# A two-layer streaming encoder on one core: reading o back before the last spill, per-chunk waits for q, and the norm roots of the first ConvFFN taken together

## The chip, the core and the metric

The kernel runs on one core of a Trainium2 chip. The metric is device time in microseconds of one execution of the whole program. Of the kernel before, three runs were timed. The core has TensorE for matmuls (PE, and PEld for its weight loads), VectorE (DVE), ScalarE (ACT), GpSimd (POOL) and SyncE (SP), each with its own instruction stream, executed in order. They wait for one another through semaphores only, and all waits are written by hand.

## The reference, cut to what matters

```python
D_MODEL, SEQ, DEPTH, DEC_SEQ, PAST_LEN = 1024, 1024, 2, 32, 256
N_HEADS, HEAD_DIM, D_FF = 16, 64, 2816

# layer 0: attention over a band of 9 chunks of 64 keys, with a relative bias
q, k, v = split(rms_norm(x, ln_mix) @ w_qkv)
o = softmax(q @ k.T * HEAD_DIM ** -0.5 + bias) @ v
x = x + o @ w_o
# layer 1 has a gMLP in its place: gelu(h @ w_in), a mix over 128 positions, @ w_out
# after either layer
a = rms_norm(x, ln_ffn) @ w_up                       # 1024 -> 5632
c = conv_b + sum(a[t - 2 + j] * conv_w[j] for j in 0, 1, 2)
gate, val = split(c)
x = x + (silu(gate) * val) @ w_down                  # 2816 -> 1024
# at the end: rms_norm(x, ln_final)
```

All data is float32. There are 1024 prompt rows and 32 sample rows. The outputs are y, the new K and V rows, the gMLP's v rows and the last rows before the convolution.

## The kernel before

**Layout.** x lies transposed in SBUF: 128 partitions, 8 feature tiles, 1056 columns (1024 prompt, 32 sample). The columns are cut into three chunks `CH` of 352 (c = 0, 1, 2). Every float32 product is made of three products of rounded parts: `product` (L158 to L160) multiplies hi by hi, lo by hi and hi by lo. `linear` runs it over 8 feature tiles, 24 matmuls of 352 columns for one output tile. The input of a matmul is `gx_hi` and `gx_lo`; weights arrive in `raw`, are rounded by ACT into `w_hi` and the rest is written by DVE into `w_lo` (a "split").

**Attention.** The 16 heads go in 8 pairs t = 0 to 7 (`PAIRS`, `LAST` = 7). Each pair has 9 steps s (`STEPS`): 8 blocks of 128 query rows and the sample block, and g = 9t + s counts all 72 steps (`ALL`). In step g PE does `scores(g)` (into PSUM banks 0 to 3), `weigh(g - 2)` (probabilities by v, into bank 6), `turn(g - 1)` (transposes of probabilities) and one output tile for the next pair, `projection(t, s)`, into bank 7. The nine tiles of a projection are v, k and q in that order, three chunks each (`divmod(s, NCH)`); DVE scales each into place and counts it in `lin_out`. The softmax of a step runs through DVE (`maxima`: bias, maximum), ACT (`exps`) and DVE (`scale`). ACT and DVE split the output o of a step into hi and lo (`high`, `low`; `low` counts `o_out`). PE waits for `lin_out` at STEPS * (t + 1) before `scores` of step 0 of a pair, that is, for all nine tiles.

**o on its way to Wo.** For pairs 0 to 6, POOL stores o_hi and o_lo into a scratch tensor in HBM, in three pieces of 384, 384 and 288 columns: `spill(t, i)` for i = 0, 1, 2. The last piece of a pair is stored at the start of the next pair's turn of the POOL loop. After the loop, `back(c)` for c = 0, 1, 2 reads the o of pairs 0 to 6 into tiles 0 to 6 of gx_hi and gx_lo, which the projections read until then; it waits for `qkv_done` (the last projection that reads chunk c) and for `spilled`. The o of pair 7 is written straight into tile 7. `back(c)` is two DMAs of 1.2 MB, counted in `o_back[c]`.

**Wo.** In pair 7 there is no next pair to project. From step 1 on, `filler(d)` computes one tile of o @ w_o for chunk 0 in that place, in bank 7; `filler(0)` first waits for `o_back[0]`. Fillers 0 to 3 leave tile 7 out, and `short(d)` adds it later. After the steps come the sixteen late tiles of chunks 1 and 2 (`for i in range(2 * KT)`), alternating banks 6 and 7, each added to x by DVE (`add`). Ahead of them PE waits for `o_out` at ALL, the lo part of the very last o. Bank 6 holds that o too. ACT and DVE write the norm's inputs of the finished x (`act_tile`, `dve_tile`), and POOL sums the squares.

**The first ConvFFN.** An iteration takes 4 weight units of 128 columns (u = 0 to 3: gate, value, gate, value) by 3 chunks: 12 "up" tiles into a ring of 6 banks, then 24 "down" tiles of 6 matmuls each. In the first iteration the tile order is (0,c0), (1,c0), (0,c1), (1,c1), (0,c2), (1,c2), (2,c0), (2,c1) and so on; o numbers them 0 to 11. For each up tile DVE evicts the bank (L1586, times rstd, counted in `free`), ACT and DVE compute the convolution (L1527, L1596, L1599), ACT takes the silu of a gate (L1532), DVE the product of a value (L1607), and both split it into h_hi and h_lo (L1488, L1564). A down chunk waits for its h_lo. rstd has to be made here: `nb_columns` on PE (sums over partitions, L300), `nb_inverse` on DVE with `nb_roots` on ACT in its middle (mean, square root, reciprocal, diagonal), `nb_spreads` on PE (L329), `nb_rstd` on ACT (L335); group 0 is the first half of the columns, group 1 the rest. The splits of units 2 and 3 and of the two down units (4, 5) are written into this order by the table `SPLITS`. In layer 0 the split of unit 2 is done at o = 0, that of unit 3 at o = 6.

## Time and profile before

| | us |
|---|---|
| runs, median (lowest to highest) | 2581.31 (2580.66 to 2583.95) |
| the profiled execution | 2582.81 |
| its span | 2581.0 |
| PE busy | 2504.8 (97%) |
| DVE busy | 1512.8 (59%) |
| ACT busy | 893.5 (35%) |
| POOL busy | 258.5 (10%) |

The profile is one execution. Its times count from the first instruction; the span leaves out 1.8 us around it. The chain of work that ended last lies on PE for 89% of the span, so the rows to read are those where PE waits and those of the granted clock: TensorE runs at one of two levels, 2.4 GHz (1.0) and 1.2 GHz (0.5), and over the whole span the mean was 0.988.

### The profile page before, as it was taken

To read this page: it belongs to the slowest core of one execution; us is meant where nothing else is said; L and a number is where in the kernel's file an instruction comes from. 1 tells how busy PE (TensorE), PEld (TensorE's weight loads), DVE (VectorE), ACT (ScalarE), POOL (GpSimd) and SP (SyncE) were. 2 spreads that over 40 slices of the span, in tenths; PEclk is the share of its full clock that TensorE was granted. 3 is DMA by queue.
4 is the path that set the end of the run, shared out by engine and by line. 5 is a ranking of instruction groups with operands and counts; after the bars stand their busy time and mean duration, and the time that the engine had idled before them with its cause. 6 is when DMAs were issued, how large, how long until landed. Compare 5 with 4: busy or idle time off the path is not lost.

```text
span 2581.0 us, 42736 instructions
## 1 busy us (share of the span) xinstructions
PE 2504.8 (97%) x16343; PEld 2427.8 (94%) x16343; DVE 1512.8 (59%) x2833; ACT 893.5 (35%) x1665; POOL 258.5 (10%) x569
## 2 busy tenths in 40 slices
PE   7999999979899999999999999999999999999998
PEld 7888888769899999999999899999999999999998
DVE  4555555556666666666665524244766666666666
ACT  5444444434522222223333530233323333222223
POOL 0111111112200000000000420221000000000003
PEclk9999999989999999999999999999999999999999
DMA  6122222264111111111111210111111111111012
GB/s 155 57 58 58 58 58 60 62 173 124 65 38 45 45 36 49 49 49 49 49 49 33 61 39 17 51 33 49 50 50 49 49 49 49 49 45 37 34 48 77
DMA packets 136980, 145.29 MB, mean 56 GB/s; under 512 B 4940, under 2 KB 126452, under 8 KB 136884
## 3 DMA queue, kind: packets, MB, share of 16 engines
q1 hardware_dynamic: 121844, 118.82, 14.4%
q0 software_dynamic: 14384, 23.03, 3.4%
q10 hardware_dynamic: 656, 2.12, 0.2%
q8 instruction: 66, 1.08, 0.2%
q14 instruction: 30, 0.25, 0.0%
HBM read 125.97 MB, written 17.97 MB: 56 GB/s over the span
## 4 chain that ended last, share of the span: by engine, by line
PE 89%; DVE 5%; ACT 3%; POOL 2%; issue 1%; DMA 1%; ACTq 0%; POOLq 0%; DVEq 0%
PE psum L158 26%; PE psum L160 26%; PE psum L159 26%; PE psum L996 2%; PE psum L1017 2%; PE psum L979 2%; POOL total L229 1%; PE psum L1848 1%; DVE gx_lo L217 1%; PE psum L898 0%; DVE w_lo L763 0%; ACT conv_t L1527 0%; ACT w_hi L759 0%; DVE gx_lo L2007 0%; PE psum L1836 0%
## 5 line engine op out<-in xcount | busy, mean ns | idle before, releaser
L158 PE MATMUL psum<-gx_hi,w_hi 128*128 128x352 f32 x3456 | 1132.9, 328 | 36.8 <-issue 12.6
L159 PE MATMUL psum<-gx_lo,w_hi 128*128 128x352 f32 x3456 | 1120.5, 324 | 0.0
L160 PE MATMUL psum<-gx_hi,w_lo 128*128 128x352 f32 x3456 | 1119.3, 324 | 0.0
L158 PEld LDWEIGHTS psum<-gx_hi,w_hi 128*128 128x128 f32 x3456 | 653.4, 189 | 42.9 <-issue 26.4
L159 PEld LDWEIGHTS psum<-gx_lo,w_hi 128*128 128x128 f32 x3456 | 654.0, 189 | 0.9 <-issue 0.7
L160 PEld LDWEIGHTS psum<-gx_hi,w_lo 128*128 128x128 f32 x3456 | 653.7, 189 | 0.0
L1623 DVE TENSOR_TENSOR x<-x,psum 128x352 f32<-128x352 f32 x528 | 258.9, 516 | 123.0 <-PE psum L160 123.0
L1527 ACT ACTIVATE conv_t<-a_gate,cur 128x352 f32<-128x352 f32 x132 | 90.2, 683 | 535.9 <-DVE a_gate L1586 535.6
L158 PE MATMUL psum<-h_hiA,w_hi 128*128 128x352 f32 x528 | 172.2, 326 | 4.3 <-DVE x L1623 4.3
L158 PE MATMUL psum<-h_hiB,w_hi 128*128 128x352 f32 x528 | 172.4, 327 | 0.0
L160 PE MATMUL psum<-h_hiB,w_lo 128*128 128x352 f32 x528 | 171.9, 326 | 0.0
L160 PE MATMUL psum<-h_hiA,w_lo 128*128 128x352 f32 x528 | 171.4, 325 | 0.0
L159 PE MATMUL psum<-h_loA,w_hi 128*128 128x352 f32 x528 | 170.6, 323 | 0.0
L159 PE MATMUL psum<-h_loB,w_hi 128*128 128x352 f32 x528 | 170.4, 323 | 0.0
L1411 DVE TENSOR_TENSOR w_lo<-raw,w_hi 128x1024 fp32r<-128x1024 f32 x132 | 161.0, 1220 | 11.0 <-ACT w_hi L1408 11.0
L1586 DVE TENSOR_TENSOR a_gate<-psum,rstd 128x352 f32<-128x352 f32 (+2 forms) x176 | 72.0, 430 | 143.3 <-PE psum L160 137.5
L1408 ACT ACTIVATE w_hi<-raw 128x1024 fp32r<-128x1024 f32 x132 | 136.0, 1044 | 5.6 <-DMA raw<-in_f_w_up 5.6
L1596 DVE SCALAR_TENSOR_TENSOR conv_t<-a_gate,cur,conv_t 128x352 f32<-128x352 f32 x132 | 77.4, 586 | 96.0 <-ACT conv_t L1527 95.8
L1527 ACT ACTIVATE conv_t<-a_val,cur 128x352 f32<-128x352 f32 x132 | 90.2, 683 | 101.8 <-DVE a_val L1586 101.8
L1532 ACT ACTIVATE s_gate<-conv_t 128x352 f32<-128x352 f32 x132 | 65.9, 499 | 165.1 <-DVE conv_t L1599 165.1
L1596 DVE SCALAR_TENSOR_TENSOR conv_t<-a_val,cur,conv_t 128x352 f32<-128x352 f32 x132 | 77.3, 586 | 72.0 <-ACT conv_t L1527 71.8
L1670 POOL COPY tails<-a_gate 128x2 f32 (+1 forms) x88 | 13.9, 190 | 928.5 <-DVE a_gate L1586 928.5
(189 smaller groups left out, 2989.3 us busy)
## 6 DMA issues: line engine op xcount, KB each, us to landing
raw<-in_f_w_up SPq DMA_DIRECT2D x44, 1024.0 KB, 5.0
raw<-in_f_w_down SPq DMA_DIRECT2D x22, 1024.0 KB, 4.8
raw<-in_a_w_o SPq DMA_DIRECT2D x25, 512.0 KB, 3.8
raw<-in_a_w_qkv SPq DMA_DIRECT2D x24, 512.0 KB, 3.7
raw<-in_b_w_in SPq DMA_DIRECT2D x8, 1024.0 KB, 5.5
raw<-in_b_w_out SPq DMA_DIRECT2D x4, 1024.0 KB, 5.2
gx_hi<-o_scratch POOLq DMA_DIRECT2D x3, 1232.0 KB, 10.7
gx_lo<-o_scratch POOLq DMA_DIRECT2D x3, 1232.0 KB, 12.9
```

Source lines behind the costliest of these rows:

```text
L158: pe.matmul(out, w[0], rhs[0], start=first, stop=False)
L159: pe.matmul(out, w[0], rhs[1], start=False, stop=False)
L160: return pe.matmul(out, w[1], rhs[0], start=False, stop=last)
L979: mm = pe.matmul(psum[:, 2 * h + i, :m], q_tok[par][HEAD_ROWS[h], P * s:P * (s + 1)], kT[par][HEAD_ROWS[h], first + m * i:first + m * (i + ...
L996: mm = pe.transpose(psum[:rows, GROUP_BANK[i], P * (2 * j + h):P * (2 * j + h + 1)], probs[g % 2][h][:, at:at + rows], ident[:, :])
L1408: act.activation(shape(f_hi[slot]), self.raw_of(u), ACT.Copy).then_inc(self.w_hi, 1)
L1411: dve.tensor_tensor(shape(f_lo[slot]), self.raw_of(u), shape(f_hi[slot]), ALU.subtract)\
L1527: act.activation(conv_t[:, o % 2, :m], a_buf[g][:, start + 2:start + 2 + m], ACT.Identity, scale=cur[:, 2, g, i:i + 1], bias=cur[:, 3, g, ...
L1532: act.activation(s_gate[:, start:start + m], conv_t[:, o % 2, :m], ACT.Silu).then_inc(self.silu, 1)
L1586: mm = dve.tensor_tensor(a_buf[g][:, at:at + b - a], psum[:, o % RING, a - start:b - start], rstd[:, a:b], ALU.mult)
L1596: dve.scalar_tensor_tensor(t, a_buf[g][:, start + 1:start + 1 + m], cur[:, 1, g, i:i + 1], t, ALU.mult, ALU.add).then_inc(self.conv1, 1)
L1623: mm = dve.tensor_tensor(chunk(x[:, d, :], c), chunk(x[:, d, :], c), psum[:, n % RING, :CH[c][1]], ALU.add)
```

## The change

The change touches five places.

- POOL: `back(0)` is issued in the turn of pair 6, after `spill(6, 1)`, and `back(1)` at the end of that turn, both ahead of `spill(6, 2)`. `back(2)` stays.
- PE: `scores` of a pair waits for the q of chunk 0 in step 0, for chunk 1 in step 2 and for chunk 2 in step 5.
- PE and DVE: the late Wo tiles take bank 7 first, then 6. The wait for `o_out` at ALL moves ahead of the second tile; the first waits for a smaller count before its last feature tile.
- The first ConvFFN, layer 0, norm: PE takes the column sums of group 0 at o = 2 (before: 4), spreads group 0 and sums group 1 at o = 4 (before: 5 and 6), spreads group 1 at o = 5 (before: 7). DVE makes both inverses ahead of the first eviction, and ACT both sets of roots.
- The same place, weights: unit 3 is split at o = 2 (before: 6).

```diff
--- before.py
+++ after.py
@@ -882,10 +882,13 @@
             pool.wait_ge(kv_copied, extras_to(g + 6))
             store_v(t + 1)
             spill(t, 1)
+            if t == LAST - 1:
+                back(0)
             pool.wait_ge(kv_copied, extras_to(g + 8))
             store_k(t + 1)
-        for c in range(NCH):
-            back(c)
+            if t == LAST - 1:
+                back(1)
+        back(2)
 
     def extra_pe(pe, e, par_next, bank):
         out = psum[:, bank, :]
@@ -921,6 +924,10 @@
     def first_extra(pe, n):
         at_least(pe, kv_copied, n - 1)
         extra_pe(pe, FIRST_EXTRAS[n], 0, 4 + n % 2)
+
+
+    QUERY_CHUNK = {0: 0, 2: 1, 5: 2}
+    assert all(P * (s + 1) <= CH[max(c for r, c in QUERY_CHUNK.items() if r <= s)][0] + 352 for s in range(NB))
 
     O_PIECE = [(0, 3 * P), (3 * P, 6 * P), (6 * P, TW)]
 
@@ -970,8 +977,8 @@
                     pe.matmul(psum[:, 2 * h, PAST:n], q_tok[par][HEAD_ROWS[h], SMP:], kT[par][HEAD_ROWS[h], SMP:],
                               start=True, stop=True).then_inc(qk_done, 1)
                 return
-            if s == 0:
-                pe.wait_ge(lin_out, STEPS * (t + 1))
+            if s in QUERY_CHUNK:
+                pe.wait_ge(lin_out, STEPS * t + 2 * NCH + QUERY_CHUNK[s] + 1)
             parts = 2 if n > BANK else 1
             m = n // parts
             for i in range(parts):
@@ -1087,15 +1094,20 @@
                     pe.wait_ge(kc_in, 16 * (t + 1))
                 extra_pe(pe, extra_at(g), (t + 1) % 2, 6)
 
-        pe.wait_ge(o_out, ALL)
         for i in range(2 * KT):
             n = WO + WO_ROWS + 1 + i
             c = 1 + i // KT
             if i % KT == 0:
                 pe.wait_ge(o_back[c], 32)
-            pe.wait_ge(at_added, max(KT, C0_DONE + i - 1) if i > 1 else KT)
+            if i == 1:
+                pe.wait_ge(o_out, ALL)
+            pe.wait_ge(at_added, C0_DONE + i - 1 if i > 1 else KT)
             pe.wait_ge(at_lo, n + 1)
-            linear(pe, psum[:, 6 + i % 2, :CH[c][1]], f_hi[unit_slot(n)], f_lo[unit_slot(n)], c).then_inc(wo_done, 1)
+            out, hi, lo = psum[:, 7 - i % 2, :CH[c][1]], f_hi[unit_slot(n)], f_lo[unit_slot(n)]
+            linear(pe, out, hi, lo, c, None, range(LAST), False)
+            if i == 0:
+                pe.wait_ge(o_out, STEPS * LAST + LAST_BLOCK[c] + 1)
+            linear(pe, out, hi, lo, c, None, range(LAST, KT)).then_inc(wo_done, 1)
 
     def attention_act(act, norm):
         act.wait_ge(qkv_done, 5)
@@ -1289,7 +1301,7 @@
                 ffn[0].split(None, dve, 0, 0)
             if i:
                 norm.dve_tile(dve, *divmod(i - 1, KT))
-            add(C0_DONE + i, 1 + i // KT, i % KT, 6 + i % 2)
+            add(C0_DONE + i, 1 + i // KT, i % KT, 7 - i % 2)
         norm.dve_tile(dve, 1, KT - 1)
         ffn[0].split(None, dve, 0, 1)
         for d in range(KT):
@@ -1413,6 +1425,7 @@
 
         SPLITS = {3: 2, 6: 3, 7: 4, 8: 5}
         NEXT_SPLITS = {2: 0, 7: 1}
+        EARLY_SPLITS = ((2, 3), (2,))
 
         def pe(self, pe, banks_free, beside=lambda e, n: None):
             ring = RING
@@ -1421,10 +1434,13 @@
                 done = self.done + it
                 for o, (u, c) in enumerate(self.items(first)):
                     if first and self.layer == 0:
-                        if o in (4, 6):
-                            nb_columns(pe, (o - 4) // 2)
-                        elif o in (5, 7):
-                            nb_spreads(pe, ((0,), (1, 2))[(o - 5) // 2])
+                        if o == 2:
+                            nb_columns(pe, 0)
+                        elif o == 4:
+                            nb_spreads(pe, (0,))
+                            nb_columns(pe, 1)
+                        elif o == 5:
+                            nb_spreads(pe, (1, 2))
                     elif first and o in self.norm_at:
                         stage = self.norm_at.index(o)
                         if stage == 0:
@@ -1493,18 +1509,20 @@
                 for o, (u, c) in enumerate(items):
                     g, i = u % 2, u // 2
                     start, n = CH[c]
-                    if o in self.SPLITS and not (first and self.SPLITS[o] == 2):
+                    if o in self.SPLITS and not (first and self.SPLITS[o] in self.EARLY_SPLITS[self.layer]):
                         self.split(act, None, it, self.SPLITS[o])
                     if o and items[o - 1][0] % 2:
                         value_hi(done, *items[o - 1])
                     if first and o == 0 and self.layer == 0:
                         nb_roots(act, 0)
                         nb_rstd(act, (0,))
+                        nb_roots(act, 1)
                         act.wait_ge(self.up, 2 * NCH - 1)
                         self.split(act, None, it, 2)
+                        nb_rstd(act, (1, 2))
                     elif first and o == 2 and self.layer == 0:
-                        nb_roots(act, 1)
-                        nb_rstd(act, (1, 2))
+                        act.wait_ge(self.up, 2 * NCH)
+                        self.split(act, None, it, 3)
                     elif first and o == 0:
                         self.norm_in.act_roots(act)
                         self.norm_in.act_spread(act, (0, 1, 2))
@@ -1573,8 +1591,9 @@
                     if first and o == 0 and self.layer == 1:
                         self.norm_in.dve_columns(dve)
                         self.split(None, dve, it, 2)
-                    if first and self.layer == 0 and o in (0, 2):
-                        nb_inverse(dve, o // 2)
+                    if first and self.layer == 0 and o == 0:
+                        nb_inverse(dve, 0)
+                        nb_inverse(dve, 1)
                     if first and self.layer == 0 and u == 0:
                         dve.wait_ge(nb_ready, 2 * c + 1 if c < 2 else 3)
                     elif first and u == 0:
@@ -1586,8 +1605,8 @@
                         mm = dve.tensor_tensor(a_buf[g][:, at:at + b - a], psum[:, o % RING, a - start:b - start],
                                                rstd[:, a:b], ALU.mult)
                     mm.then_inc(self.free, 1)
-                    if first and o == 0 and self.layer == 0:
-                        self.split(None, dve, it, 2)
+                    if first and o in (0, 2) and self.layer == 0:
+                        self.split(None, dve, it, 2 + o // 2)
                     if o and items[o - 1][0] % 2:
                         value_lo(done, *items[o - 1])
                     m = CONV_N[c]
@@ -1608,7 +1627,7 @@
                                                    conv_t[:, o % 2, cut.start - start:cut.stop - start],
                                                    s_gate[:, cut], ALU.mult)
                         mm.then_inc(self.prod, 1)
-                    if o in self.SPLITS and not (first and self.SPLITS[o] == 2):
+                    if o in self.SPLITS and not (first and self.SPLITS[o] in self.EARLY_SPLITS[self.layer]):
                         self.split(None, dve, it, self.SPLITS[o])
                 value_lo(done, *items[-1])
                 at_least(dve, self.added, DOWN * done)
```

In the rows of the order, line numbers after the change are 10 to 20 higher than before from the first ConvFFN on (L1408 is L1420, L1411 is L1423, L1527 is L1545, L1532 is L1550, L1564 is L1582, L1586 is L1605, L1596 is L1615, L1607 is L1626).

The order of POOL's DMAs from the third `store_k` row on, before and after (o_scratch<-o_hi 128x288 is `spill(6, 2)`, gx_hi<-o_scratch is a `back`):

```order
L843 DMA out_2<-kout 128x4x128
L845 DMA out_4<-kout 32x128
L853 DMA o_scratch<-o_hi 128x288
L853 DMA o_scratch<-o_lo 128x288
L834 DMA vc<-in_cache_a_v 128x2x128
L862 DMA gx_hi<-o_scratch 128x7x352
L862 DMA gx_lo<-o_scratch 128x7x352
L862 DMA gx_hi<-o_scratch 128x7x352
L862 DMA gx_lo<-o_scratch 128x7x352
L862 DMA gx_hi<-o_scratch 128x7x352
L862 DMA gx_lo<-o_scratch 128x7x352
```

```order
L862 DMA gx_hi<-o_scratch 128x7x352
L862 DMA gx_lo<-o_scratch 128x7x352
L843 DMA out_2<-kout 128x4x128
L845 DMA out_4<-kout 32x128
L862 DMA gx_hi<-o_scratch 128x7x352
L862 DMA gx_lo<-o_scratch 128x7x352
L853 DMA o_scratch<-o_hi 128x288
L853 DMA o_scratch<-o_lo 128x288
L834 DMA vc<-in_cache_a_v 128x2x128
L862 DMA gx_hi<-o_scratch 128x7x352
L862 DMA gx_lo<-o_scratch 128x7x352
```

Two of the three read-backs have moved ahead of the store of kout, and of the last spill with the load of vc.

ACT at the start of the first ConvFFN, before and after (L321 is a square root, w_hi<-raw a split, L335 rstd; the rows begin after the last square):

```order
L321 ACT_TABLE_LOAD
L321 ACTIVATE rs_col<-rs_col 128x4
L335 ACTIVATE rstd<-psum 128x512
L1408 ACTIVATE w_hi<-raw 128x1024
L1527 ACTIVATE conv_t<-a_gate,cur 128x352
L1532 ACT_TABLE_LOAD
L1532 ACTIVATE s_gate<-conv_t 128x352
L1527 ACTIVATE conv_t<-a_val,cur 128x352
L1488 ACTIVATE h_hiA<-prod 128x352
L321 ACT_TABLE_LOAD
L321 ACTIVATE rs_col<-rs_col 128x4
L321 ACTIVATE rs_col<-rs_col 32x1
```

```order
L321 ACT_TABLE_LOAD
L321 ACTIVATE rs_col<-rs_col 128x4
L335 ACTIVATE rstd<-psum 128x512
L321 ACTIVATE rs_col<-rs_col 128x4
L321 ACTIVATE rs_col<-rs_col 32x1
L1420 ACTIVATE w_hi<-raw 128x1024
L335 ACTIVATE rstd<-psum 128x512
L335 ACTIVATE rstd<-psum 128x32
L1545 ACTIVATE conv_t<-a_gate,cur 128x352
L1550 ACT_TABLE_LOAD
L1550 ACTIVATE s_gate<-conv_t 128x352
L1545 ACTIVATE conv_t<-a_val,cur 128x352
```

The second square roots now follow the first without a table load between, the split of unit 2 stands behind them and ahead of the second rstd.

DVE in the same place, from the first product (prod) on, before and after:

```order
L1607 TENSOR_TENSOR prod<-conv_t,s_gate 128x352
L307 TENSOR_SCALAR rs_col<-psum 128x4
L307 TENSOR_SCALAR rs_col<-psum 32x1
L311 RECIPROCAL rs_col<-rs_col 128x4
L311 RECIPROCAL rs_col<-rs_col 32x1
L315 TENSOR_SCALAR total<-ident,rs_col 128x128 x4
L315 TENSOR_SCALAR total<-ident,rs_col 32x32
L1586 TENSOR_TENSOR a_gate<-psum,rstd 128x352
L1564 TENSOR_TENSOR h_loA<-prod,h_hiA 128x352
L1596 SCALAR_TENSOR_TENSOR conv_t<-a_gate,cur,conv_t 128x352
```

```order
L1626 TENSOR_TENSOR prod<-conv_t,s_gate 128x352
L1605 TENSOR_TENSOR a_gate<-psum,rstd 128x352
L1423 TENSOR_TENSOR w_lo<-raw,w_hi 128x1024
L1582 TENSOR_TENSOR h_loA<-prod,h_hiA 128x352
L1615 SCALAR_TENSOR_TENSOR conv_t<-a_gate,cur,conv_t 128x352
```

The means, reciprocals and diagonals of group 1 are gone from here; the split of unit 3 (w_lo<-raw,w_hi) has come in behind the next eviction.

## Rows read from the trace of the kernel before

**Rows 1.** Page part 1, then waits of PE: waited for: us in total, times, longest.
```profile
PE 2504.8 (97%) x16343; PEld 2427.8 (94%) x16343; DVE 1512.8 (59%) x2833; ACT 893.5 (35%) x1665; POOL 258.5 (10%) x569
...
PE psum L158 <- issue: 12.6, 1, 12.6
...
PE psum L979 <- DVE q L1203: 5.0, 7, 0.7
```
**Rows 2.** Timeline of PE: start, duration, what, [idle before <- who ended it].
```profile
450.44 0.32 PE L160 MATMUL psum<-gx_hi,w_lo 128*128 128x352 f32 x1
450.68 0.49 PE L979 MATMUL psum<-kT,q 64*128 64x256 f32 x2
...
506.29 0.32 PE L160 MATMUL psum<-gx_hi,w_lo 128*128 128x352 f32 x1
507.32 0.49 PE L979 MATMUL psum<-kT,q 64*128 64x128 f32 x4 [0.71 <-DVE q L1203]
...
513.81 0.33 PE L996 MATMUL psum<-ident,pB 128*128 128x128 f32 x1
526.72 0.63 PE L158 MATMUL psum<-gx_hi,w_hi 128*128 128x352 f32 x1 [12.58 <-issue]
...
532.20 0.92 PE L979 MATMUL psum<-kT,q 64*128 64x384 f32 x4
```
**Rows 3.** Timeline of POOL's DMA issues around the read-back.
```profile
496.60 0.56 POOL L853 DMA_DIRECT2D o_scratch<-o_hi  x1 [11.02 <-DVE o_lo L1242]
...
518.12 0.96 POOL L862 DMA_DIRECT2D gx_lo<-o_scratch  x1
```
**Rows 4.** DMA issued from 518 to 519: KB each, median us to landing.
```profile
gx_lo<-o_scratch POOLq DMA_DIRECT2D x1, 1232.0 KB, 8.5
```
**Rows 5.** Stretches: us, PE, PEld, DVE, ACT, POOL busy (count), PE clock, DMA share, GB/s.
```profile
514.00:514.20 0.20, 0.14 (x1) 0.00 (x0) 0.20 (x1) 0.02 (x1) 0.00 (x0) 0.50 0.54 92
...
592.50:595.90 3.40, 3.40 (x13) 3.40 (x13) 0.13 (x1) 0.00 (x0) 0.00 (x0) 0.51 0.55 157
703.30:708.50 5.20, 5.20 (x18) 5.20 (x19) 3.66 (x7) 3.10 (x5) 0.43 (x3) 0.50 0.61 202
```
**Rows 6.** Timeline of DVE, then of PE, at the first late Wo tile.
```profile
588.29 1.23 DVE L763 TENSOR_TENSOR w_lo<-raw,w_hi 128x1024 fp32r<-128x1024 f32 x1 [2.22 <-ACT w_hi L759]
...
591.39 0.43 PE L158 MATMUL psum<-gx_hi,w_hi 128*128 128x352 f32 x1 [2.78 <-DVE gx_lo L1242]
```
**Rows 7.** Timeline of PE in the first ConvFFN iteration.
```profile
670.75 0.95 PE L300 MATMUL psum<-ones,total 128*128 128x2 f32 x8
671.55 0.41 PE L158 MATMUL psum<-gx_hi,w_hi 128*128 128x352 f32 x1
...
675.49 1.02 PE L329 MATMUL psum<-total,ones 128*128 128x512 f32 x2
...
680.21 1.10 PE L300 MATMUL psum<-ones,total 128*128 128x2 f32 x10
...
686.85 1.46 PE L329 MATMUL psum<-total,ones 128*128 128x512 f32 x4 [1.49 <-DVE total L315]
...
703.30 0.66 PE L158 MATMUL psum<-gx_hi,w_hi 128*128 128x352 f32 x1 [7.11 <-DVE w_lo L1411]
...
717.26 0.32 PE L158 MATMUL psum<-h_hiA,w_hi 128*128 128x352 f32 x1
```
**Rows 8.** Timeline of ACT: the split of unit 2, ahead of the first convolution.
```profile
677.04 1.05 ACT L1408 ACTIVATE w_hi<-raw 128x1024 fp32r<-128x1024 f32 x1
```
**Rows 9.** Timeline of DVE in the same iteration.
```profile
683.34 0.21 DVE L307 TENSOR_SCALAR rs_col<-psum 128x4 f32<-128x4 f32 x2
...
690.01 0.58 DVE L1596 SCALAR_TENSOR_TENSOR conv_t<-a_gate,cur,conv_t 128x352 f32<-128x352 f32 x1 [0.32 <-ACT conv_t L1527]
...
714.06 0.52 DVE L1564 TENSOR_TENSOR h_loB<-prod,h_hiB 128x352 fp32r<-128x352 f32 x1
...
721.65 0.94 DVE L1623 TENSOR_TENSOR x<-x,psum 128x352 f32<-128x352 f32 x2
```

## The prediction

> **What bounds the kernel now.** I read the page's busy shares first, then PE's list of waits, then the timeline of PE at each of them, and last the granted clock of the stretches around. PE is busy 97% of the span [rows 1], so only time in which PE stands still or runs at the lower clock can be won. The largest single wait is one of 12.6 us that the list puts down to "issue". The timeline has it at the first filler of pair 7: work on PE ends at 514.14 and goes on at 526.72 [rows 2]. What came just then is the second DMA of `back(0)`: issued at 518.12 [rows 3], landed 8.5 us later [rows 4], at 526.62. Next are 7 waits of 0.7 us for the last q tile, one for each pair from 1 to 7 [rows 1, 2], a wait of 2.78 us for the very last o_lo [rows 6], and two in the first iteration of the first ConvFFN, 1.49 us for the diagonals and 7.11 us for the w_lo of unit 3 [rows 7]. After three of these waits TensorE worked at 1.2 GHz for a while [rows 5]. All five parts of the change lie on one of these waits; nothing else of the program moves.
>
> **Read-back, at the start of pair 7.** `back(0)` needs the projection of chunk 0 (done well before pair 6's step 7) and the first piece, stored long before. So it is issued right behind `spill(6, 1)`, whose first DMA stands at 496.60 [rows 3]: two issues of 0.56 us, then two of 0.96. The last of these begins at about 498.7, and with the same 8.5 us to landing it is there at 507.2, while `filler(0)` could start at 513.9. Cover: 6.7 us; each microsecond of landing beyond costs one. Passed on POOL: the store of kout and, with `back(1)`, `spill(6, 2)` and the load of vc. POOL stood idle for 11.02 us ahead of the row at 496.60, and the store of kout is late by no more than the two issues, 2 us; nobody on the path waits for it before the first ConvFFN. `back(1)` and `back(2)` are wanted only at the late Wo tiles, 70 us on. They move 2.5 MB each beside matmuls, as `back(1)` and `back(2)` do now.
> What it is worth: `filler(0)` starts at 526.72 and the next scores at 532.20 [rows 2]. At full clock the 21 matmuls of a filler take 3.4 us (21 x 0.161; 24 matmuls stand in the 3.94 us from 671.55 to 675.49 [rows 7], 0.09 of it the restart), so the scores would stand at 513.9 + 3.4 + 0.25 = 517.5: **14.7 us**. Of these 12.6 are the wait, the rest nearly all the lower clock in its wake. But the lower level was granted from 514.0 on [rows 5], before the long wait had begun: what came ahead of it was the thin start of pair 7, whose two waits for the softmax stay. A low stretch of 3.4 us, as at 592.5 [rows 5], costs 12 matmuls x (0.29 - 0.16) = 1.6 us. I take it as coming again: **13.1**, bounds 12.6 and 14.7.
>
> **Scores wait by chunk.** The last projection matmul starts at 506.29, the scores at 507.32, a distance of 1.03; at step 1 it is 0.24 (450.44 to 450.68) [rows 2]. So 0.79 us goes at each of the pairs 1 to 6, whose later steps show no wait on PE: the next tile's 24 matmuls hide the softmax, which moves up too. 6 x 0.79 = 4.7. In pair 7 step 0 has no such tile and the softmax chain binds; it starts when DVE has evicted q, 0.6 us sooner: 0.6. The two added waits of a pair (steps 2 and 5) are for counts long reached; queued behind them are only PE's own scores. **5.3**, bounds 4.4 and 5.5.
>
> **Late Wo tile.** The first tile no longer needs bank 6 or the last o_lo; next is its weight. DVE's split starts at 588.29 and takes 1.23 [rows 6]: 589.52. PE would start at 589.55 in place of 591.39: 1.84. The wait left is then 0.9 us in place of 2.78, and the low stretch from 592.5 to 595.9 held 13 matmuls [rows 5], 13 x 0.13 = 1.7 us, that I count as gone. The second tile needs the last o_lo (591.3) at 593.5. The third needs a weight whose load now has less slack; I take off 0.1. **3.4**, bounds 1.7 and 3.5.
>
> **First ConvFFN iteration: a wait removed, another in its place.** First PE, in times of the trace. The twelve up tiles end at 717.26 [rows 7]. Without the waits (1.49 and 7.11, with the restart 1.65 and 7.27) and without the low clock of 703.3 to 708.5, 18 matmuls [rows 5], 2.3 us, they end at 706.0. The sums and spreads cost the same in their new places.
> Then DVE, which runs behind. PE's fourth tile ended at 670.75. Ahead of the end of its fifth now lie the first sums (671.55 - 670.75 = 0.80), the first spread (680.21 - 675.49 - 3.85 = 0.87) and the second sums (about 1.0) [rows 7]: it ends at 677.4, so the split of unit 2, at 677.04 before [rows 8], starts at 677.7, and ACT puts the second rstd (0.7) behind it. The first convolution is later by 0.85. That is a loss, though the roots are out of the way.
> At 683.34 DVE began the second inverse; the convolution of the third tile followed at 690.01 [rows 9]: 6.7 us. In its place stand an eviction (0.45), ACT's h_hi and split (1.5, partly beside it), DVE's split (1.14) and h_lo (0.5): 3.3 us. Net: 690.01 + 0.85 - 3.35, **2.5 us sooner**. Taking DVE's split of unit 3 out of o = 6 gives nothing more: ACT's split of unit 4 precedes the next convolution there, as before.
> So the h_lo that the first down tile needs, at 714.06 before [rows 9], comes at 714.06 - 2.5 - 0.3 (a wait for PE that goes) = 711.3, done at 711.8. PE has waited there since 706.0: **5.8 us take the place of the 7.11**. It starts the down tiles at 711.8 in place of 717.26, 5.4 sooner. The waits of 2.78 and 7.11 were both followed by work at the lower clock [rows 5]; with the same 2.3 us it leaves **3.1**. Without it DVE binds: its additions start at 717.9 in place of 721.65 [rows 9], the third is done at 720.4 after a split, and the ninth down tile starts with it, 4.6 sooner. With a longer low stretch 2.0; the DVE chain itself may be off by 0.5. Bounds 1.5 and 4.6.
>
> **The sum.** 13.1 + 5.3 + 3.4 + 3.1 = 24.9. The profiled execution took 2582.81, so it would be 2557.9; that execution is 1.5 above the median of 2581.31. For the median I predict **2556.4**. All bounds one way: 27.7 + 0.4, 2553.2; the other way: 12.6 + 4.4 + 1.7 + 1.5 = 20.2, 2561.1.
>
> **Rivals.**
> *Clock.* The low stretch at pair 7 stays away, and so does the one before the down tiles: 14.7 + 5.3 + 3.4 + 4.6 = 28.0, 2553.3. For it: with the chain 5 us sooner the thin start may fall otherwise. Against it: the same thin work, and 5.8 us of standing.
> *ConvFFN gives nothing.* DVE can't evict until both inverses are through, and ACT's split waits for PE's fifth tile. If this costs 3 us more than I made it, the part is worth 0: 2559.5. For it: I add up ten pieces on three engines. Against it: each has a duration in the trace.
> *The 12.6 us are not the read-back's.* The list says "issue", not DMA. If another thing held PE (a weight, an eviction), the part is worth at most 1: 24.9 - 12.1, 2568.5. Against it: the landing at 526.62 and the start at 526.72 agree to 0.1 us.
> *Slower.* POOL writes the DMAs of `back` itself. Before, it did so from 517.1 to 523.0, when DVE had nothing to do; now it does so from 497.7, between DVE's scalings and evictions. If POOL were held off there, the landing would slip. It decides at 513.9: the gain is gone, and the kernel slower than before by 0.2%, when `back(0)` lands 24.9 + 5 us later than that, at 544, against 507 expected. For it speaks no row: the spills at 496.60 were issued beside DVE's work in 0.56 us each. If the four issues stretched by all of DVE's scalings there (some 2 us) they would still be covered. Time if it held: 2587.
> The Trainium skill has this as a rule against the change: "SBUF - State Buffer", section "Who interferes with whom", says that a DVE instruction in a two-port mode and GpSimd shut each other out for whole instructions, tensor_scalar among them, so that descriptors for a DMA from GpSimd are written late. By that rule up to four scalings of about 0.5 us fall on the four issues; the landing moves from 507.2 to 509 and the sum stays. No row of the trace before shows a `back` issued beside a scaling.
>
> **Chances.** The forecast's case 0.64, both clocks better 0.12, ConvFFN nothing 0.15, not the read-back 0.05, slower 0.02, and 0.02 for a loss elsewhere that leaves no change. The range goes from 2552.8 to 2561.5, the bounds of the sum with a little for the median of few runs; it leaves out the last three and the tails. About 0.2%, 5 us, is what a measurement of this kernel can tell from no change. Faster by more than that: 0.95; within: 0.03; slower: 0.02.
>
> **What would show it.** The read-back: no wait on PE at `filler(0)`, the issue of `back(0)` at about 493 in times of the new trace, landed before PE needs it. Clock: one low stretch of some 3.4 us at the start of pair 7, none at the first late Wo tile. Scores: PE's waits for q gone from the list; in pair 7 the waits for pB stay. Late Wo: a wait of 0.9 us for w_lo (L763) in place of 2.78. ConvFFN: no wait for w_lo at the first tile of unit 3, and a wait of about 5.8 us for h_lo ahead of the first down tile. Wrong it would be if PE stood at `filler(0)` for more than 1 us, if the first down tile came without a wait, or if the waits of pair 7 for the softmax grew.

## The result, and the profile after

The changed kernel takes 2556.81 us (median of 4 runs, 2556.66 to 2557.63). The kernel before took 2582.63 us (4 runs, 2580.66 to 2584.04: the three whose median was 2581.31, and one more). The ratio is 0.990, with a 95% interval of 0.9887 to 0.9912: 25.8 us less. Predicted were 2556.4, with a range of 2552.8 to 2561.5.

The busy times of the profiled execution, and TensorE's longest waits (which line waits <- for whom: us in total, times, longest), as [rows 1] has them of before:

```profile
span 2555.1 us, 42749 instructions
PE 2500.5 (98%) x16343; PEld 2424.3 (95%) x16343; DVE 1513.9 (59%) x2833; ACT 890.7 (35%) x1663; POOL 258.8 (10%) x569
```
```profile
PE psum L158 <- DVE gx_lo L217: 6.7, 6, 2.6
PE psum L498 <- DMA par_rows<-in_ln_final: 6.3, 1, 6.3
PE psum L1003 <- DVE pB L1265: 5.9, 7, 1.5
PE psum L158 <- issue: 5.5, 1, 5.5
```

The 12.6 us at "issue" are gone, and so are the seven waits for q. A new wait stands at "issue", 5.5 us long. ScalarE runs two instructions fewer, both loads of its function tables, since the square roots now stand together. Line numbers below are those of the changed kernel, in which what stood behind line 890 stands 3 to 19 lines further down.

**Start of pair 7.** TensorE's timeline (start, duration, engine and line, what, [idle before <- who ended it]), to be held against [rows 2]:

```profile
502.83 0.32 PE L160 MATMUL psum<-gx_hi,w_lo 128*128 128x352 f32 x1
503.08 0.49 PE L986 MATMUL psum<-kT,q 64*128 64x128 f32 x4
...
506.61 0.70 PE L986 MATMUL psum<-kT,q 64*128 64x256 f32 x4 [0.99 <-ACT pB L1142]
...
509.41 0.33 PE L1003 MATMUL psum<-ident,pA 128*128 128x128 f32 x1 [1.51 <-DVE pB L1265]
...
509.60 0.41 PE L158 MATMUL psum<-gx_hi,w_hi 128*128 128x352 f32 x1
...
510.39 0.49 PE L158 MATMUL psum<-gx_hi,w_hi 128*128 128x352 f32 x1
510.69 0.49 PE L159 MATMUL psum<-gx_lo,w_hi 128*128 128x352 f32 x1
...
514.70 0.59 PE L986 MATMUL psum<-kT,q 64*128 64x384 f32 x2
```

The scores at 503.08 stand 0.25 us behind the last projection matmul, where 1.03 lay before. The filler at 509.60 follows the turns at once, where before it waited 12.58 us. Its matmuls are 0.30 us apart for a while (510.39 to 510.69), which is the 1.2 GHz level; the granted clock of the stretch is 0.50 (columns as in [rows 5]):

```profile
509.90:513.30 3.40, 3.40 (x13) 3.40 (x12) 1.64 (x6) 1.39 (x5) 1.86 (x3) 0.50 0.95 263
```

All 13 matmuls are the filler's, twelve of them at the slow spacing. The two waits for the softmax (0.99 and 1.51) are left.

From the scores at step 0 to those at step 2 the time is 11.62 us (514.70 - 503.08), against 24.88 before (532.20 - 507.32): 13.3 us less.

GpSimd's issues there, to be held against [rows 3]:

```profile
493.15 0.56 POOL L853 DMA_DIRECT2D o_scratch<-o_hi  x1 [11.03 <-DVE o_lo L1254]
493.70 0.54 POOL L853 DMA_DIRECT2D o_scratch<-o_lo  x1
494.23 1.00 POOL L862 DMA_DIRECT2D gx_hi<-o_scratch  x1
495.23 0.98 POOL L862 DMA_DIRECT2D gx_lo<-o_scratch  x1
496.63 0.78 POOL L843 DMA_DIRECT2D out<-kout  x1 [0.43 <-ACT kout L912]
```

The second DMA of `back(0)`, issued at 495.23, landed after

```profile
gx_lo<-o_scratch POOLq DMA_DIRECT2D x1, 1232.0 KB, 9.9
```

that is at 505.1, 4.5 us ahead of the filler's start at 509.60. Before it took 8.5 [rows 4].

**First late Wo tile**, to be held against [rows 6]: the wait for the last o_lo has given way to one for the weight, and the tile behind it runs at 2.4 GHz (the granted clock of the stretch is 1.00; columns as in [rows 5]).

```profile
572.18 0.40 PE L158 MATMUL psum<-gx_hi,w_hi 128*128 128x352 f32 x1 [1.05 <-DVE w_lo L763]
```
```profile
572.10:576.00 3.90, 3.82 (x24) 3.85 (x25) 3.05 (x6) 1.22 (x3) 0.48 (x1) 1.00 0.45 134
```

**First ConvFFN iteration.** TensorE, to be held against [rows 7], then VectorE and ScalarE, to be held against [rows 8, 9]:

```profile
656.42 1.35 PE L329 MATMUL psum<-total,ones 128*128 128x512 f32 x4
...
684.54 0.32 PE L160 MATMUL psum<-gx_hi,w_lo 128*128 128x352 f32 x1
690.38 0.63 PE L158 MATMUL psum<-h_hiA,w_hi 128*128 128x352 f32 x1 [5.51 <-issue]
```
```profile
652.58 0.21 DVE L307 TENSOR_SCALAR rs_col<-psum 128x4 f32<-128x4 f32 x2 [4.52 <-PE psum L300]
...
654.28 0.51 DVE L1605 TENSOR_TENSOR a_gate<-psum,rstd 128x352 f32<-128x352 f32 x1
657.71 1.23 DVE L1423 TENSOR_TENSOR w_lo<-raw,w_hi 128x1024 fp32r<-128x1024 f32 x1 [2.93 <-ACT w_hi L1420]
658.85 0.58 DVE L1615 SCALAR_TENSOR_TENSOR conv_t<-a_gate,cur,conv_t 128x352 f32<-128x352 f32 x1
...
662.49 0.53 DVE L1626 TENSOR_TENSOR prod<-conv_t,s_gate 128x352 f32<-128x352 f32 x1
...
689.75 0.52 DVE L1582 TENSOR_TENSOR h_loB<-prod,h_hiB 128x352 fp32r<-128x352 f32 x1
```
```profile
656.62 1.06 ACT L1420 ACTIVATE w_hi<-raw 128x1024 fp32r<-128x1024 f32 x1 [3.50 <-PE psum L160]
```

The up tiles end at 684.7 without a wait. Then TensorE stands until 690.38. The list has this wait under "issue"; the h_lo that the tile needs starts at 689.75 and ends at 690.27, 0.11 us ahead of it. The chain of VectorE behind that h_lo has a hole near its start: VectorE evicts output 0 at 654.28, and then has nothing to do for 2.93 us, because its next instruction is its half of unit 2's split. That waits for ScalarE's half, and ScalarE in turn for TensorE's fifth tile. The down tiles begin at 1.2 GHz (columns as in [rows 5]):

```profile
690.30:694.20 3.90, 3.83 (x13) 3.85 (x14) 3.49 (x8) 1.22 (x3) 0.59 (x2) 0.50 0.09 29
```

Where the time went, by the same place in both traces. Of the column sums of group 0 the place is taken where they stand after, ahead of the third up tile; before, that tile starts there at 663.07. The start of execution is 1.1 us slower in the profile after (a low-clock stretch at 42 us twice as long), which no edit touches, so distances are taken from step 1's scores of pair 0.

| stretch | before less after, us | predicted |
|---|---|---|
| step 1 of pair 0 to step 0 of pair 7 | 5.3 | 5.3 |
| pair 7, step 0 to step 2 | 13.3 | 13.1 |
| to the second late Wo tile | 3.3 | 3.4 |
| to the third up tile of the first ConvFFN (after: to the column sums ahead of it) | 0.3 | 0 |
| to the end of its first iteration | 4.0 | 3.1 |
| rest of the program | 0.8 | 0 |
| start of execution | -1.1 | 0 |

### The profile page after: what moved, and what is told of

Read it like the earlier page. It is cut to its first block, busy times and chain, and to the rows that moved or that the text cites. A ratio compares the mean times of both kernels' runs of the same rounds, so it can differ in the third digit from the quotient of the medians.

```text
span 2555.1 us, 42749 instructions
## 1 busy us (share of the span) xinstructions
PE 2500.5 (98%) x16343; PEld 2424.3 (95%) x16343; DVE 1513.9 (59%) x2833; ACT 890.7 (35%) x1663; POOL 258.8 (10%) x569
## 4 chain that ended last, share of the span: by engine, by line
PE 89%; DVE 5%; ACT 3%; POOL 2%; issue 1%; DMA 0%; ACTq 0%; DVEq 0%; POOLq 0%
PE psum L158 26%; PE psum L160 26%; PE psum L159 26%; PE psum L1003 2%; PE psum L1024 2%; PE psum L986 2%; POOL total L229 1%; PE psum L1867 1%; DVE gx_lo L217 1%; PE psum L901 0%; ACT conv_t L1545 0%; DVE w_lo L763 0%; DVE conv_t L1615 0%; DVE conv_t L1618 0%; ACT w_hi L759 0%
## 5 line engine op out<-in xcount | busy, mean ns | idle before, releaser
L1545 ACT ACTIVATE conv_t<-a_gate,cur 128x352 f32<-128x352 f32 x132 | 90.1, 683 | 535.4 <-DVE a_gate L1605 535.3
L1423 DVE TENSOR_TENSOR w_lo<-raw,w_hi 128x1024 fp32r<-128x1024 f32 x132 | 161.2, 1221 | 13.9 <-ACT w_hi L1420 13.9
L1605 DVE TENSOR_TENSOR a_gate<-psum,rstd 128x352 f32<-128x352 f32 (+2 forms) x176 | 72.0, 430 | 137.4 <-PE psum L160 137.4
L1420 ACT ACTIVATE w_hi<-raw 128x1024 fp32r<-128x1024 f32 x132 | 136.0, 1044 | 8.4 <-DMA raw<-in_f_w_up 4.9
L1615 DVE SCALAR_TENSOR_TENSOR conv_t<-a_gate,cur,conv_t 128x352 f32<-128x352 f32 x132 | 77.4, 587 | 96.5 <-ACT conv_t L1545 96.4
L1545 ACT ACTIVATE conv_t<-a_val,cur 128x352 f32<-128x352 f32 x132 | 90.1, 683 | 100.5 <-DVE a_val L1605 100.5
L1550 ACT ACTIVATE s_gate<-conv_t 128x352 f32<-128x352 f32 x132 | 65.9, 499 | 166.9 <-DVE conv_t L1618 166.9
L1615 DVE SCALAR_TENSOR_TENSOR conv_t<-a_val,cur,conv_t 128x352 f32<-128x352 f32 x132 | 77.4, 586 | 71.5 <-ACT conv_t L1545 71.3
L158 PEld LDWEIGHTS psum<-h_hiA,w_hi 128*128 128x128 f32 x528 | 100.3, 190 | 10.6 <-issue 7.6
```

Of the source, the lines that this page charges most:

```text
L158: pe.matmul(out, w[0], rhs[0], start=first, stop=False)
L1420: act.activation(shape(f_hi[slot]), self.raw_of(u), ACT.Copy).then_inc(self.w_hi, 1)
L1423: dve.tensor_tensor(shape(f_lo[slot]), self.raw_of(u), shape(f_hi[slot]), ALU.subtract)\
L1545: act.activation(conv_t[:, o % 2, :m], a_buf[g][:, start + 2:start + 2 + m], ACT.Identity, scale=cur[:, 2, g, i:i + 1], bias=cur[:, 3, g, ...
L1550: act.activation(s_gate[:, start:start + m], conv_t[:, o % 2, :m], ACT.Silu).then_inc(self.silu, 1)
L1605: mm = dve.tensor_tensor(a_buf[g][:, at:at + b - a], psum[:, o % RING, a - start:b - start], rstd[:, a:b], ALU.mult)
```

## The experiments

The theory is that of the prediction: each part is worth the wait that it removes and the low clock behind that wait, and what stays in the first ConvFFN iteration is VectorE's chain. The rivals are those of the prediction: the 12.6 us are not the read-back's, a part only shifts its wait, or the low clock comes whatever the wait is. Four kernels undo one part each, two more divide the last part, and five try to take away what is left of it. Two numbers are given for each: the median, and the distance D from step 1's scores of pair 0 to the end of the first ConvFFN's first iteration, from the trace. D holds all five parts of the change and neither the start nor the end of the program. It is 667.8 us before and 641.6 in the changed kernel; in a second profile of the changed kernel it is 641.6 again. It is not free of chance either: in the twelve profiles without the long wait the low-clock stretch at pair 7 is 3.4 us long eight times and 6.8 four times, and those four kernels differ from the changed kernel only behind it. The longer one adds 0.9 to 1.2 us to D. So step 0 to step 2 of pair 7 (11.62 us in the changed kernel) is looked at beside D.

**Read-back undone.** All three read-backs behind the loop:

```diff
-            if t == LAST - 1:
-                back(0)
...
-            if t == LAST - 1:
-                back(1)
-        back(2)
+        for c in range(NCH):
+            back(c)
```

> The changed kernel with the read-back of o undone: back(0), back(1) and back(2) are all written after the loop again. Theory (the read-back is worth 13.3 us of the 25.8): median 2570.1 (2556.8 + 13.3), the wait of 12.6 us ahead of the score blocks of pair 7 stands again between filler(0) and step 2, the 3.4 us of low clock behind it stay as they are with and without. DVE's two scalings that took 0.95 and 1.05 us beside GpSimd's issues of back(0) take 0.55 again. Rival (the 12.6 us is not the read-back's but GpSimd's queue or q's): median 2556.8 to 2558 and the wait as short as in the changed kernel, or the scalings still near 1.0.

Measured: 2568.86 us, ratio 0.9945 (0.9928 to 0.9961); D longer by 12.8. The wait is back:

```profile
PE psum L158 <- issue: 17.9, 2, 12.4
```

Here 12.4 of the 17.9 us are the filler's and 5.5 the down tile's. VectorE's scalings, which had been stretched, are short again. First the changed kernel, then this one:

```profile
494.57 0.95 DVE L1265 TENSOR_SCALAR pA<-pA,row_inv 128x640 f32<-128x640 f32 x1
495.44 1.05 DVE L1265 TENSOR_SCALAR pB<-pB,row_inv 128x640 f32<-128x640 f32 x1
```
```profile
493.08 0.56 DVE L1262 TENSOR_SCALAR pA<-pA,row_inv 128x640 f32<-128x640 f32 x1
493.55 0.55 DVE L1262 TENSOR_SCALAR pB<-pB,row_inv 128x640 f32<-128x640 f32 x1
```

The wait was the read-back's, and its order is worth half of the change. The second rival (the 12.6 us are not the read-back's) is out.

**Chunk wait undone.** One wait for all of q at step 0:

```diff
-            if s in QUERY_CHUNK:
-                pe.wait_ge(lin_out, STEPS * t + 2 * NCH + QUERY_CHUNK[s] + 1)
+            if s == 0:
+                pe.wait_ge(lin_out, STEPS * (t + 1))
```

> The changed kernel with one wait for all of q at step 0 of each pair, in place of one per query chunk. Theory (each of 7 pairs loses 0.78 us, and pair 7 no more than that): median 2562.3 (2556.8 + 5.5), step 0 of pairs 1 to 7 waits 0.6 to 0.8 us each. Rival A (the wait is only shifted to the end of the pair, where keys are waited for): median 2556.8 to 2557.5. Rival B (in pair 7 a later start also moves the read-back's issues, and some of the 4.5 us by which the landing leads is lost): more than 5.5.

Measured: 2560.76 us, ratio 0.9913 (0.9897 to 0.993); D longer by 5.1, and the seven waits in the list as before:

```profile
PE psum L986 <- DVE q L1215: 5.0, 7, 0.7
```

Step 0 of pair 7 comes 5.3 us later, counted from pair 0. The median shows 4.0 only, and the two profiled executions differ by 3.3 (2560.19 against 2556.86): the start of execution took 1.1 us less here, and all that stands behind the first iteration 0.7 less. A large piece of the second is a stretch that no edit touches: from the end of the first iteration to the gated mixing the program took 799.4 us here and 801.0 in the changed kernel. In the fourteen traces it takes 799.4 to 799.5 us five times, 801.0 eight times and 800.2 once. The granted clock tells them apart. All eight with 801.0 have a low-clock stretch of 3.4 us that starts 711 to 713 us behind the end of the iteration, and the five with 799.5 don't have it. One that starts at 688 to 690 us stands in all of the five and in five of the eight, and shows no cost. What makes the later one come is not shown. So a median can't weigh one part of a few us; D can do it better.

**Late Wo tile undone.** Banks and waits as before:

```diff
+        pe.wait_ge(o_out, ALL)
         for i in range(2 * KT):
...
-            out, hi, lo = psum[:, 7 - i % 2, :CH[c][1]], f_hi[unit_slot(n)], f_lo[unit_slot(n)]
+            out, hi, lo = psum[:, 6 + i % 2, :CH[c][1]], f_hi[unit_slot(n)], f_lo[unit_slot(n)]
```

> The changed kernel with the late Wo tiles as before: banks 6, 7 in turn, and the wait for the whole of o's norm ahead of the first tile. Theory: the first late tile waits 2.8 us again for gx_lo (1.05 for w_lo in the changed kernel) and 3.4 us of low clock stand behind it again, which cost 1.6: median 2560.1 (2556.8 + 3.3). Rival A (the wait alone, the clock comes low by chance): 2558.6. Rival B (what is late is only moved into FFN, whose own wait ahead of the first down tile takes it in): 2556.8.

Measured: 2559.48 us, ratio 0.9907 (0.989 to 0.9923); D longer by 3.1. Both halves of the price are back, the wait and the low clock behind it (the order of the banks and the place of the wait were not undone one by one):

```profile
573.68 0.43 PE L158 MATMUL psum<-gx_hi,w_hi 128*128 128x352 f32 x1 [2.78 <-DVE gx_lo L1250]
```
```profile
574.10:577.40 3.30, 3.30 (x14) 3.30 (x12) 0.82 (x1) 0.00 (x0) 0.00 (x0) 0.50 0.55 164
```

**The ConvFFN part undone, whole and by halves.** Three kernels: norm order and unit 3's split as before; only the split as before; only the norm order as before. The split's edit, then the norm's (TensorE's side):

```diff
-        EARLY_SPLITS = ((2, 3), (2,))
+        EARLY_SPLITS = ((2,), (2,))
...
-                        if o == 2:
-                            nb_columns(pe, 0)
-                        elif o == 4:
-                            nb_spreads(pe, (0,))
-                            nb_columns(pe, 1)
-                        elif o == 5:
-                            nb_spreads(pe, (1, 2))
+                        if o in (4, 6):
+                            nb_columns(pe, (o - 4) // 2)
+                        elif o in (5, 7):
+                            nb_spreads(pe, ((0,), (1, 2))[(o - 5) // 2])
```

> The changed kernel with the first ConvFFN iteration as before: both norm groups at outputs 4 to 7, the second roots behind the first evictions, unit 3 split at output 6. Theory: 4.0 us come back, median 2560.8; TensorE waits some 7 us for unit 3's low part ahead of output 9 and hardly at all ahead of the first down tile, which starts 5.8 us later against the first columns than in the changed kernel. Rival (the chain of VectorE ends where it did, the iteration gives nothing): 2556.8.

Measured: 2561.57 us, ratio 0.9918 (0.9901 to 0.9934); D longer by 3.5.

> The changed kernel with the norm groups as changed, but unit 3 split at output 6 as before. Theory (VectorE's chain of evictions and convolutions ends last, wherever the split stands in it): TensorE waits 5.5 us for unit 3's low part ahead of output 9 and about 0 ahead of the first down tile, which starts where it does in the changed kernel (690.4, 0.5 either way); median 2556.8, 1 us either way. Rival (the early split is what the iteration gains by): the 5.5 us are paid twice, 2560 to 2562.

Measured: 2556.52 us, ratio 0.9895 (0.9878 to 0.9911); D shorter by 0.4. TensorE's wait stands elsewhere and is 4.2 us long:

```profile
677.91 0.43 PE L158 MATMUL psum<-gx_hi,w_hi 128*128 128x352 f32 x1 [4.15 <-DVE w_lo L1423]
```

> The changed kernel with both norm groups and the roots where they stood before (sums at outputs 4 and 6, spreads at 5 and 7, the second roots behind the first evictions), but unit 3 split at output 2 as changed. Theory (the norm's order is what moved VectorE's chain, the split only moves where TensorE stands): up tiles without a wait for unit 3's low part, the first down tile some 5 us later than in the changed kernel (695.4) with a wait of 9 to 10 us ahead of it; median 2560.8 to 2561.5, as with both undone. Rival (the early split gives the iteration part of its 4 us): 2558 to 2559.

Measured: 2560.04 us, ratio 0.991 (0.9894 to 0.9927); D longer by 4.7. No wait for unit 3, but

```profile
693.70 0.63 PE L158 MATMUL psum<-h_hiA,w_hi 128*128 128x352 f32 x1 [7.74 <-issue]
```

So the four microseconds of this part are the norm order's. The early split of unit 3 moves TensorE's wait from output 9 to the first down tile, and in the traces it costs time. With it undone D is shorter by 0.4 us only because pair 7 had its longer low-clock stretch there (12.60 us from step 0 to step 2 in place of 11.62); from the first column sums to the end of the iteration the kernel with the late split takes 72.0 us, the changed one 73.6. The first down tile starts within 0.2 us of the same place in both. But with the late split the low clock (678.2 to 681.6) lies on up tiles, where it takes time that TensorE would have waited, and the down tiles take 23.4 us; with the early split it lies on the down tiles, and they take 25.1. With the norm order as before it is the same: D is 1.2 us longer with the early split (4.7) than without (3.5), and the down tiles take 26.0 us against 23.4. Each of these is one trace, and the medians (2556.52 against 2556.81, 2561.57 against 2560.04) don't show it. The wait of 7.74 was 1 to 2 us shorter than expected, because 1.50 us of it stood elsewhere again, ahead of the second spreads as in [rows 7].

**What holds VectorE's chain?** The hole of 2.93 us names the split of unit 2. The first kernel moves the convolution of output 0 into the hole (ScalarE's side; on VectorE the split goes behind the eviction of output 1):

```diff
                         nb_roots(act, 1)
+                        affine(0)
                         act.wait_ge(self.up, 2 * NCH - 1)
                         self.split(act, None, it, 2)
                         nb_rstd(act, (1, 2))
+                        affine(1)
+                        silu(0)
```

> The changed kernel, and in its first ConvFFN iteration ScalarE's affine of output 0 stands ahead of the split of unit 2, its affine of output 1 ahead of the first silu, and VectorE's half of that split behind the eviction of output 1 in place of 0. Theory: VectorE waited 2.93 us for the split's high part with nothing else to do, now it convolves output 0 in that time; the product of output 1 comes 1.7 us sooner (662.49 to 660.8), the first down tile waits 3.8 us in place of 5.5: median 2555.1. Rival A (TensorE's own tiles set VectorE's pace, 1.7 us of it are taken back by later waits for them): 2556.8. Rival B (unit 2's low part is late for output 6, PE stalls): 2557 to 2558.

Measured: 2555.13 us, ratio 0.989 (0.9873 to 0.9906); D shorter by 1.3; the wait ahead of the first down tile is 4.04 us:

```profile
688.16 0.63 PE L158 MATMUL psum<-h_hiA,w_hi 128*128 128x352 f32 x1 [4.04 <-issue]
```

The second leaves the convolutions and brings the norm's second sums forward (on ScalarE the second rstd then stands ahead of the split of unit 2):

```diff
-                        elif o == 4:
-                            nb_spreads(pe, (0,))
+                        elif o == 3:
+                            pe.wait_ge(nb_mean, 1)
                             nb_columns(pe, 1)
-                        elif o == 5:
-                            nb_spreads(pe, (1, 2))
+                        elif o == 4:
+                            nb_spreads(pe, (0, 1))
+                        elif o == 5:
+                            nb_spreads(pe, (2,))
```

> The changed kernel with the second norm group's sums at output 3 in place of 4, the spreads of the first two pieces together at output 4 and the last at output 5; nothing else moved. Theory: evict of output 0 comes 2 us sooner (654.3 to 652.2), but its convolution still stands behind the split of unit 2 and the roots, which wait for output 4's end: the chain gains nothing, the first down tile waits 5.5 us as before, median 2556.8, 0.7 either way. Rival (the second group's roots and spreads hold the chain, not the split): 2 us less, 2554.8.

Measured: 2557.48 us, ratio 0.99 (0.9884 to 0.9917); D longer by 2.1, of which some 1 us was a longer low-clock stretch. Output 0 was evicted sooner, at 653.53, for nothing. One spread more lay ahead of TensorE's fifth tile, so the split of unit 2 began at 657.60 in place of 656.62:

```profile
657.60 1.06 ACT L1420 ACTIVATE w_hi<-raw 128x1024 fp32r<-128x1024 f32 x1 [3.25 <-PE psum L160]
```

and the wait ahead of the first down tile grew by the same microsecond, to 6.36. The split of unit 2, and through it TensorE's fifth tile, holds the chain, and the norm doesn't.

The third has both edits:

> Both of the two kernels ahead in one: sums of the second group at output 3, and the convolutions of outputs 0 and 1 ahead of or around the split of unit 2. Theory: output 0's convolution starts at 653.5 in place of 658.9 and output 1's product is ready at some 657.5 in place of 662.5; TensorE's last up tile (684.7) and the first down tile then meet within 0.7 us, so that nearly all of the 5.5 us and the 1.7 us of low clock behind it go: median 2550 to 2551. Rival A (TensorE's tiles set the pace from output 5 on, and the chain gains half): 2553.5. Rival B (a low-clock stretch comes whatever the wait is): 2551.5 to 2552.

Measured: 2555.84 us, ratio 0.9894 (0.9877 to 0.991); D longer by 0.8, of which 1.2 arose in pair 7, where the low-clock stretch was 6.8 us long in place of 3.4. The wait was 4.13 us, no less than with the first edit (4.04). My expectation was 5 us too low. I had put the convolution of output 0 ahead of the split, but silu(0) behind it, and silu has ScalarE load a table first. So output 1's product waited until 660.97.

The fourth puts silu(0) and affine(1) ahead of the split as well, moves VectorE's halves of both splits behind the work that was ready, and puts ScalarE's half of unit 3's split between the affine and the silu of output 2:

```diff
                         affine(0)
+                        silu(0)
+                        affine(1)
                         act.wait_ge(self.up, 2 * NCH - 1)
                         self.split(act, None, it, 2)
                         nb_rstd(act, (2,))
-                        affine(1)
-                        silu(0)
...
+                    if first and o == 2 and self.layer == 0:
+                        self.split(None, dve, it, 2)
                     for a, b, at in self.pieces(c):
...
-                    if first and o in (1, 2) and self.layer == 0:
-                        self.split(None, dve, it, 1 + o)
+                    if first and o == 3 and self.layer == 0:
+                        self.split(None, dve, it, 3)
```

> As the kernel with both edits, but outputs 0 and 1 are convolved, and output 0's silu taken, wholly ahead of the split of unit 2 on ScalarE and VectorE, unit 3's split stands between affine and silu of output 2 on ScalarE and behind the eviction of output 3 on VectorE. Theory: the product of output 1 is ready at 658.4 to 658.9 in place of 661.0, that of output 3 at 665.5 to 666 in place of 668.2; the wait ahead of the first down tile falls from 4.1 to 1.4 us: median 2.7 us under that kernel's, 2553.1. Rival (the low-clock stretch there stays, and takes in what the shorter wait gives): 2554.5 to 2555.5.

Measured: 2553.96 us, ratio 0.9887 (0.9871 to 0.9904); D shorter by 3.4, though its pair 7 again had the longer low-clock stretch, for 1.2 us more. The wait is 1.17 us, and the low-clock stretch that had come in this iteration in every kernel so far is gone. Beside it on the same chip ran the changed kernel once more:

> The changed kernel itself once more, beside the two above on the same chip: 2556.8, 0.7 either way; its second profile says how much of the program's parts is chance (the start of execution has moved by up to 1.5 us between profiles, and the end by as much).

Measured: 2556.99 us, ratio 0.9899 (0.9883 to 0.9916). The fourth kernel beats it by 3.0 us, and its slowest run (2554.49) is faster than the changed kernel's fastest (2555.81).

The last takes the earlier sums away again and keeps the order of convolutions and splits:

> The order of the kernel that came to 2553.96 us, with outputs 0 and 1 convolved ahead of the split of unit 2 and unit 3's split behind output 2's affine, but the norm's sums and spreads where the changed kernel has them (second sums at output 4). Theory (the order of convolutions and splits is what earns the gain; the earlier sums only let output 0 be evicted sooner, and cost TensorE 0.6 us in switches): output 0 is evicted at 654.3 and output 1's product is ready at 659.6, as in that kernel within 0.2 us of the changed kernel's time; the wait ahead of the first down tile is 1.8 us (1.17 there, with up tiles that end 0.6 later); median 2553.5 to 2554. Rival (without the earlier sums silu's table load collides with the split of unit 2 again): wait 3 to 4 us, median 2555 to 2556.

Measured: 2552.59 us, ratio 0.9877 (0.986 to 0.9893), a little under the 2553.5 expected; one of its four runs took 2548.01. D is shorter by 3.8, with the longer low-clock stretch at pair 7 here too (0.9 us). ScalarE, then TensorE, then the granted clock of what follows:

```profile
655.17 0.68 ACT L1527 ACTIVATE conv_t<-a_gate,cur 128x352 f32<-128x352 f32 x1 [1.70 <-DVE a_gate L1620]
655.87 1.28 ACT L1534 ACT_TABLE_LOAD   x1
657.16 0.50 ACT L1534 ACTIVATE s_gate<-conv_t 128x352 f32<-128x352 f32 x1
657.56 0.67 ACT L1527 ACTIVATE conv_t<-a_val,cur 128x352 f32<-128x352 f32 x1
658.14 1.05 ACT L1420 ACTIVATE w_hi<-raw 128x1024 fp32r<-128x1024 f32 x1
```
```profile
686.92 0.40 PE L158 MATMUL psum<-h_hiA,w_hi 128*128 128x352 f32 x1 [1.71 <-issue]
```
```profile
684.70:690.00 5.30, 3.59 (x23) 3.33 (x22) 4.74 (x11) 2.30 (x4) 0.59 (x2) 1.00 0.51 176
```

The wait of 1.71 us is what was expected (1.8). The table load now runs while VectorE convolves output 0, and costs nothing. This is the lowest median of the study, 30.4 us under the kernel before on the same chip (2583.03) and some 4 us under the changed kernel. From the fourth kernel, whose D is 0.4 us longer, its runs don't set it apart; but it needs fewer edits, so the earlier sums earn nothing. Both keep the early split of unit 3; whether they would do better without it was not tried.

## Why the prediction was right, point by point

**Read-back: right.** Predicted 13.1, in the trace 13.3, by undoing it 12.8. The low-clock stretch that I took as coming again came: 3.4 us, 12 matmuls. The issues began within 0.1 us of the place that the steps gave (497.7 in times of before); the "about 493" of the signs was 1.2 too early (494.23), because the start of execution took 1.1 us longer. The cover was 4.5 us, and not 6.7: the landing took 9.9 instead of 8.5, and the filler stood ready 0.8 us earlier against its pair than I had it. Neither cost anything.

**Chunk scores wait: right.** 0.79 for a pair was predicted; each of pairs 1 to 7 gives 0.78, and together with a loss of 0.2 in pair 0 that makes 5.3. In pair 7 the softmax chain moved up with q as forecast, by a little more than the 0.6 I had allowed.

**Late Wo tile: right.** 3.4 predicted, 3.3 in the trace. The wait left is 1.05 us for w_lo (0.9 predicted), and the low stretch stayed away.

**First ConvFFN iteration: right mechanism, term too small by 0.9.** The steps held one by one. Against the first column sums, the split of unit 2 started at the time predicted (656.6), the third tile's convolution at 666.1 (666.4 predicted), and the up tiles ended at 684.7 (684.9). The h_lo came at 689.75 (690.2 predicted), so the wait that takes the place of the 7.11 was 5.5 and not 5.8 us, and the first down tile came 5.8 us sooner against the column sums and not 5.4. The larger error is the price of the clock: I let 18 matmuls run at 1.2 GHz as before, and 13 did, 1.7 us in place of 2.3. That makes 5.8 - 1.8 = 4.0 in place of 5.4 - 2.3 = 3.1, the 1.8 being these 1.7 and 0.1 of rounding. One statement of the working was sharper than I had used it: taking VectorE's half of unit 3's split out of output 6 "gives nothing more". The whole early split gives nothing, and in the two pairs of traces with and without it it costs 1.2 to 1.5 us, with the low clock on the down tiles each time it is there and on up tiles each time it is not. So the price that I took off at the down tiles belongs, by these traces, to a piece of the change itself.

**The rivals.** Of the clock's two gains neither came, so the 2553.3 of that case did not come; and the first ConvFFN iteration gave 4.0 where its rival had 0. The slower rival was put down to GpSimd being held off while it writes the DMAs of `back`. In the trace two scalings do fall on the issues, and the issues take 1.00 and 0.98 us, as the quiet ones before did (0.96 [rows 3]). It was VectorE that was held: 0.95 and 1.05 in place of 0.56 and 0.55, 0.9 us in all, at a place where TensorE had other work. The Trainium skill, "SBUF — State Buffer", section "Who interferes with whom", says that issue order decides who blocks. GpSimd's issue began first here (494.23 against 494.57), so the side that is held agrees. It also says that the first gets the shared pair of ports for its whole instruction, and that the row does not bear out: the first scaling ended 0.3 us after the first issue did, with the second issue already under way, which a scaling of 0.55 us that starts only at 495.23 could not have done.

**What the sum missed, and the luck in it.** The median came out 0.4 us above the number predicted, closer than the sum deserved. The two traces differ by 25.9 us and not by 24.9: ConvFFN's 0.9, 0.3 between the late Wo tiles and the column sums and 0.8 in the rest of the program came beyond the sum, 1.1 at the start of execution was lost, and pair 7 and the late tile make up the last 0.1. The sum was taken from the median of three runs, 2581.31; the fourth run moved that median to 2582.63, and from there 24.9 less would have been 2557.7. That the 1.0 us beyond the sum and the low median of three runs (1.3 us) nearly cancel is luck. The moves outside the edits are chance of the kind that the second profile of the changed kernel shows: its start took 0.6 us more again. One sum was also added wrong: the four upper bounds give 28.3 us and not 28.1, that is 2553.0 in place of 2553.2, which the stated range holds too.

## What to carry to other kernels

When a wait goes, follow the engine that was behind it back to its first idle time: here the 5.5 us that remained were made in one hole of 2.93 us, 30 us earlier, where an instruction that could run stood behind one that could not. An order that helps one engine's wait may only move it, to a place where it costs more (unit 3's split), so undo each half of a part alone before believing in it. Weigh small parts by a distance in the trace that brackets the edits, and look for low-clock stretches inside it; the medians carried 1 to 2 us from places no edit touched, and D up to 1.2.
